# One transfer of 2 MB for each expert weight matrix, in place of two of 1 MB

## What is computed

```
def expert_block(args):
    xb, e = args
    return (jax.nn.silu(xb @ w_gate[e]) * (xb @ w_up[e])) @ w_down[e]
# w_gate, w_up: (32, 1024, 512); w_down: (32, 512, 1024), float32: 2 MB each matrix, 6 MB an expert
```

## Time and profile before

| | |
|---|---|
| median of 3 runs | 1305.73 us (1301.58 to 1308.01) |
| the profiled execution | 1303.58 us, of which the span from first to last instruction is 1301.7 us |
| PE busy | 1159.6 us (89%) |
| DVE busy | 888.3 us (68%) |
| ACT busy | 738.4 us (57%) |
| DMA queue of SP (q1) | 241.83 MB, 49.1% of the 16 engines' time |
| DMA queue of ACT (q10) | 25.17 MB, 5.8% |
| weights of experts | 192 transfers of 1024 KB; median from issue to landing 8.2 us (down) to 9.6 us (gate) |

### The profile page before, as it was taken

How to read it: one execution, slowest core, us unless ns; L and a number is a source line. 1 busy time by engine, 2 the same in 40 slices (tenths; PEclk the granted TensorE clock), 3 DMA queues, 4 the chain that set the end, 5 groups by cost and what they waited for, 6 DMA issues and landing times. The chain is left out here.

```text
span 1301.7 us, 17793 instructions
## 1 busy us (share of the span) xinstructions
PE 1159.6 (89%) x6109; PEld 907.0 (70%) x6109; DVE 888.3 (68%) x1117; ACT 738.4 (57%) x882; POOL 80.0 (6%) x135
## 2 busy tenths in 40 slices
PE   5999999999999997799849999999999999999930
PEld 3888788779878885588736666766666766667620
DVE  7345635543563454666668889888898888988828
ACT  7344444453444434523247777777777777777714
POOL 0011011011010000011200000000000000000013
PEclk9999999999999998899969999999999999999975
DMA  6145353355341000584359999999999999999838
GB/s 181 50 114 123 81 129 81 89 122 120 89 98 40 17 18 1 200 322 159 150 202 377 383 393 392 404 395 388 390 395 398 400 390 392 390 397 400 316 97 333
DMA packets 86215, 306.31 MB, mean 235 GB/s; under 512 B 14664, under 2 KB 39240, under 8 KB 61600
## 3 DMA queue, kind: packets, MB, share of 16 engines
q1 hardware_dynamic: 67680, 241.83, 49.1%
q0 software_dynamic: 11328, 38.80, 10.8%
q10 hardware_dynamic: 7168, 25.17, 5.8%
HBM read 254.36 MB, written 51.41 MB: 235 GB/s over the span
## 5 line engine op out<-in xcount | busy, mean ns | idle before, releaser
L1476 DVE TENSOR_TENSOR m_wl<-raw,m_wh 128x2048 fp32r<-128x2048 f32 x192 | 437.2, 2289 | 74.8 <-ACT m_wh L1350 72.3
L1350 ACT ACTIVATE m_wh<-raw 128x2048 fp32r<-128x2048 f32 x192 | 367.9, 1918 | 130.1 <-PE m_py L131 50.6
L129 PE MATMUL m_pg<-m_wh,m_xh 128*96 128x512 f32 x256 | 104.2, 407 | 6.6 <-DVE m_xl L1480 5.3
L143 PE MATMUL a_pj<-zh,a_wh 128*128 128x348 f32 (+1 forms) x416 | 107.5, 355 | 0.5 <-DVE a_wl L495 0.5
L143 PE MATMUL a_pj<-zl,a_wh 128*128 128x348 f32 (+1 forms) x416 | 107.6, 355 | 0.0
L143 PE MATMUL a_pj<-zh,a_wl 128*128 128x348 f32 (+1 forms) x416 | 106.4, 352 | 0.0
L129 PE MATMUL m_py<-m_wh,m_hh 128*96 128x512 f32 x256 | 102.5, 401 | 2.3 <-DVE m_hl L1505 2.3
L129 PE MATMUL m_pu<-m_wh,m_xh 128*96 128x512 f32 x256 | 102.7, 401 | 0.0
L131 PE MATMUL m_pg<-m_wh,m_xl 128*96 128x512 f32 x256 | 101.7, 397 | 0.0
L130 PE MATMUL m_pg<-m_wl,m_xh 128*96 128x512 f32 x256 | 101.3, 396 | 0.0
L131 PE MATMUL m_pu<-m_wh,m_xl 128*96 128x512 f32 x256 | 101.2, 395 | 0.0
(11 more groups left out here) (241 smaller groups left out, 2107.1 us busy)
## 6 DMA issues: line engine op xcount, KB each, us to landing
raw<-in_w_gate_dram SPq DMA_DIRECT2D x64, 1024.0 KB, 9.6
raw<-in_w_up_dram SPq DMA_DIRECT2D x64, 1024.0 KB, 8.9
raw<-in_w_down_dram SPq DMA_DIRECT2D x64, 1024.0 KB, 8.2
xrows<-a_kl POOLq DMA_DIRECT2D x51, 256.0 KB, 4.9
a_raw<-in_w_in_dram SPq DMA_DIRECT2D x24, 512.0 KB, 4.0
m_xg<-xrows ACTq DMA_DIRECT2D x32, 384.0 KB, 8.1
yrows<-m_ys ACTq DMA_DIRECT2D x32, 384.0 KB, 6.9
yrows<-a_kl POOLq DMA_DIRECT2D x33, 256.0 KB, 4.9
```

What stands on the lines that cost most here:

```text
L129: nc.tensor.matmul(out, xh, wh, start=first, stop=False)
L143: mm = nc.tensor.matmul(out, w[:, k, 0:m], z[:, k, at:at + n], start=n_pass == 0, stop=n_pass == PASSES - 1)
L1350: nc.scalar.activation(wh[s][:], raw[j][:], ACT.Copy).then_inc(S["w_hi"], 1)
L1476: nc.vector.tensor_tensor(wl[s][:], raw[j][:], wh[s][:].bitcast(F32), ALU.subtract).then_inc(S["w_lo"], 1)
```

## The change

Each matrix becomes one transfer of 2 MB, 16 KB in each partition, into one of three staging buffers `big[0]` to `big[2]`. The units stay as they were for ACT, DVE and PE: `raw[j]` is now the first or second half of `big[j // 2]`. Both halves' `high` wait for the landing of the whole matrix, and SP waits for the `low` of the second half before it issues the next transfer into the buffer. The transfers ahead in the router stage are three instead of six, with the same bytes in the same order.

```diff
-                        for e, kind, j in [(0, 0, 2), (0, 1, 3), (0, 2, 4), (0, 3, 5), (1, 0, 0), (1, 1, 1)]:
-                            to, src = unit(c.raw[j], kind, e, w_gate, w_up, w_down)
+                        for e, m, j in [(0, 0, 1), (0, 1, 2), (1, 0, 0)]:
+                            to, src = matrix(c.big[j], m, e, w_gate, w_up, w_down)
                             sp.dma_start(to, src).then_inc(c.raw_in[j], 16)
...
-def unit(raw, j, e, w_gate, w_up, w_down):
-
-    n, w = (DE, (w_gate, w_up)[j // 2]) if j < 4 else (D, w_down)
-    half = UNIT // n
-    rows = w[0, bass.ds(e, 1), :, :].rearrange("o (p k) n -> p (o k) n", p=P)
-    return raw[:].rearrange("p (k n) -> p k n", n=n), rows[:, (j % 2) * half:(j % 2 + 1) * half, :]
+def matrix(raw, m, e, w_gate, w_up, w_down):
+
+    n, w = (D, w_down) if m == 2 else (DE, (w_gate, w_up)[m])
+    return raw[:].rearrange("p (k n) -> p k n", n=n), w[0, bass.ds(e, 1), :, :].rearrange("o (p k) n -> p (o k) n", p=P)
...
-                    for kind in kinds(shift):
+
+                    for kind in kinds(shift)[::2]:
...
-                            sp.wait_ge(S["w_lo"], split(N, j - UNITS))
-                        to, src = unit(raw[j], kind, behind if kind in DOWN else e, w_gate, w_up, w_down)
-                        sp.dma_start(to, src).then_inc(raw_in[j], 16)
+                            sp.wait_ge(S["w_lo"], split(N, j + 1 - UNITS))
+                        to, src = matrix(c.big[j // 2], kind // 2, behind if kind in DOWN else e, w_gate, w_up, w_down)
+                        sp.dma_start(to, src).then_inc(raw_in[j // 2], 16)
...
-                    act.wait_ge(raw_in[j], N * 16 + (16 if j >= 2 else 0))
+                    act.wait_ge(raw_in[j // 2], N * 16 + (16 if j >= 2 else 0))
...
-            c.raw = [c.sb(ctx, f"raw{j}", [P, UNIT], F32) for j in range(UNITS)]
-            c.raw_in = [c.sem(f"first_raw_in{j}") for j in range(UNITS)]
+            c.big = [c.sb(ctx, f"raw{j}", [P, 2 * UNIT], F32) for j in range(UNITS // 2)]
+            c.raw = [c.big[j // 2][:, j % 2 * UNIT:(j % 2 + 1) * UNIT] for j in range(UNITS)]
+            c.raw_in = [c.sem(f"first_raw_in{j}") for j in range(UNITS // 2)]
```

More of the change, by code:

```diff
@@ L1217, in experts @@
                                               "y_copied", "ids_ready", "counted", "made", "placed", "collected", "listed", "own", "passed")}
-        raw_in = [c.sem(f"{tag}_raw_in{j}") for j in range(UNITS)] if dynamic else c.raw_in
+        raw_in = [c.sem(f"{tag}_raw_in{j}") for j in range(UNITS // 2)] if dynamic else c.raw_in
         gathered = [c.sem(f"{tag}_gathered{s}") for s in range(2)]
@@ L1346, in high @@
                     s = (UNITS * u + j) % RING
-                    act.wait_ge(raw_in[j], N * 16 + (16 if j >= 2 else 0))
+                    act.wait_ge(raw_in[j // 2], N * 16 + (16 if j >= 2 else 0))
                     act.wait_ge(S["unit_used"], N * UNITS + (j + 1))
-                    nc.scalar.activation(wh[s][:], raw[j][:], ACT.Copy).then_inc(S["w_hi"], 1)
+                    nc.scalar.activation(wh[s][:], raw[j], ACT.Copy).then_inc(S["w_hi"], 1)
                 def x_high(N, u):
@@ L1475, in low @@
                     dve.wait_ge(S["w_hi"], N * UNITS + (j + 1))
-                    nc.vector.tensor_tensor(wl[s][:], raw[j][:], wh[s][:].bitcast(F32), ALU.subtract).then_inc(S["w_lo"], 1)
+                    nc.vector.tensor_tensor(wl[s][:], raw[j], wh[s][:].bitcast(F32), ALU.subtract).then_inc(S["w_lo"], 1)
                 def x_low(N, u):
```

## The result

| | before | changed |
|---|---|---|
| median (22 runs each) | 1304.39 us | 1308.02 us |
| range | 1301.18 to 1309.34 | 1302.78 to 1312.27 |
| profiled execution, span | 1301.7 us | 1306.2 us |
| last matmul of the experts | 1250.4 us | 1254.6 us |

The ratio is 1.0029 with a 95% interval of 1.0018 to 1.0039: the changed kernel is slower by 3.8 us (3.6 by the medians), less than half a per cent, but clear of the noise. Measured again beside other kernels it was 1.0028 (1.0016 to 1.0040) and 1.0034 (1.0020 to 1.0049). The time lies in the range that was predicted; the forecast of no change at all, though, was wrong, and a sum of 0 us has to be explained against 4.

What follows compares the result with a forecast made beforehand. The prediction took PE to bound the experts' stage, with transfers just keeping up. Its terms summed to 0 us, giving 1305.7 us, the median of the three runs, with a range of 1299 to 1314 us.

Steps and rivals of the forecast that it cites:

- PE bounds the stage; the transfers just keep up.: Experts' stage: PE busy 99.7 of 100 us sets the pace, not the DMA share of 1.02.
- The landing: Weight transfers: the matrix's last byte arrives when now, leaving 1.8, 0.9 and 1.2 us before the first highs; cost 0.
- Runs of 16 KB: Weight transfers: longer runs were taken to move at the 8 KB rate, 426 GB/s with full queue.
- If the margin is gone: From ACT's highs to PE: a single landing may be 5.3 us late before PE stops.
- The dry bound: Weight transfers, each meeting an empty queue: landing 11.1 us, over the 17.96 us step only for UP, costing 0 to 5 us.
- The point of decision: Landing time beyond which a lost head start would cost: 11.3 us for DOWN, 10.9 us for UP and GATE.
- rival 1: Weight transfers: first half's head start lost in full, +1.4 us an expert, 43 us, 1348 us; chance 8 in 100.
- Rival 2: DMA beside ACT's row stores: mixing costs 0.95 us more an expert, 28 us, 1334 us; chance 6 in 100.
- Rival 3: Experts' stage bound by DMA: steady 426 GB/s shortens it by 39 us, 1266 us; chance 6 in 100.
- What the profile would show: Experts' stage if right: step 17.96 us, waits on PE as now, landings 9 to 11.3 us, highs 0 to 2 us later.
- Both signs of being wrong: Experts' stage: landings over 11.3 us in the steady state, or the DMA share falling while the step grows.
- The resolution: Whole-kernel timing: a measurement was said to tell about 0.5%, 6.5 us, from no change.

Runs made afterwards that it cites:

- e7: Kernel before, with ACT splitting rows between GATE's halves and DVE doing `m_xl` between GATE's two lows; ratio 0.9941, median 1295.8 us.
- e15: Kernel before with late issue of both halves and ACT waiting for both landings, still two transfers of 1 MB (a repeat); ratio 0.9998.
- e14: Changed kernel with 64 bytes between a staging buffer's halves, so one 2 MB transfer in runs of 8 KB (a repeat); ratio 1.0010.
- e13: The changed kernel again, unedited, measured on one chip beside two variants; ratio 1.0034 against the kernel before.
- e6: Changed kernel, with ACT splitting rows between GATE's halves and DVE doing `m_xl` between GATE's two lows; ratio 1.0013, step 18.01 us.
- e11: Kernel before with rows split between GATE's halves, late issue and whole landing together, two transfers of 1 MB; ratio 0.9985, step 17.85 us.
- e2: Kernel before, with only ACT's high of a first half waiting for the landing of both halves; ratio 0.9994.
- e3: Kernel before with late issue of both halves and ACT waiting for both landings, still two transfers of 1 MB; ratio 0.9987.
- e4: Changed kernel with 64 bytes between a staging buffer's halves, so one 2 MB transfer in runs of 8 KB; ratio 1.0006.
- e5: The changed kernel again, unedited, measured beside other kernels; ratio 1.0028 against the kernel before.

## Why the prediction was wrong

- *"PE bounds the stage; the transfers just keep up."* Right for PE's waits. But the way by which PE is bound was read from matmul rhythm and from the weights' slots alone. PE also waits 0.2 us at each start of GATE for `m_xl`, and no view that I used names this: the wait is shorter than what the waits' list shows for PE and stands there only as "PEld m_pg <- issue". Of the 7.7 us that e7 gains (0.59%), 6.2 lie at the 30 turns to GATE and were there to be seen, and 1.5 at the first two experts.
- *The landing: "the last byte of the matrix arrives when the second half's does now, because the bytes ahead of it are the same".* This step failed. The term was 9.0, 10.3 and 9.6 us for UP, DOWN and GATE; measured 10.4, 11.3 and 11.3. Against what was left, 1.8, 0.9 and 1.2 us, that is 1.4, 1.0 and 1.7 us more: UP keeps a margin (0.5 us in the trace), DOWN and GATE have none. With two transfers of 1 MB the step does hold: from the end of the second `low`, DOWN takes 10.6 us in e15 and 10.5 before. One transfer of 2 MB takes 11.1 us in runs of 8 KB (e14) and 11.6 in runs of 16 KB (e13).
- *"Runs of 16 KB ... I take the 8 KB rate."* Failed too, though not by the rate of the weights themselves: the row transfers on ACT's queue become late, 10.0 instead of 8.3 us, and around each row load 0.13 to 0.17 MB less is moved. The two bounds looked at the rate of the weights alone and left the other queue out. "If the hardware cuts the 16 KB up again" did not happen, as the packets show.
- *"If the margin is gone ... late by 5.3 us before PE stops."* This step failed as well and is what turned late landings into lost time. It followed the late high only to the matmuls that use those weights, and there it may well be right: the first low of GATE ends 4 us before its first matmul even in the changed kernel. On ACT the row split `m_xh` stands behind the highs of GATE, on DVE `m_xl` stands behind their lows and `m_hid`, and there the margin was 0 us, as the chain shown above tells. e6 and e7 show this way, by removing it.
- *The dry bound: 11.1 us landing at most, "0 to 5 us".* The bound was passed (11.3 to 11.5 us). The cost of 3.8 us lies within what it allowed, but by luck: the 5 us were worked out for UP, which waits for nothing. Hold and landing were the right pair to add up, for DOWN: its hold shrinks to 6.44 us when both halves are split back to back, and with 0.18 us to the issue, 11.34 to the landing and 0.10 to the high (medians of the changed kernel) the cycle has 18.06 us, the step. That says that no slack is left in it; it doesn't explain the landing.
- *The point of decision in rival 1, "a landing takes more than 11.3 us (DOWN)".* This was the right kind of number, and the changed kernel sits on it (11.3 us; with the shorter hold of 6.44 us, and 0.3 us for issue and start, the point is 11.2). The mechanism of rival 1, a lost head start, is real only together with the whole landing and only at a faster pace (e11). The price of 43 us was far too high: it took the whole delay as lost, while in e15 none of it was.
- *Rival 2, mixing with the row transfers.* Nearest to what happened, with the load instead of the store: the slow time around the load is 6 us, where it is 5 before and 4 in e14 with runs of 8 KB. The rate beside the store stays at 421 to 430 GB/s. Its price of 28 us took a loss of 0.95 us of DMA time a step; measured are 0.3 to 0.4 us (against e14), and the step grew by 0.1.
- *Rival 3* (a stage bound by DMA gains from larger transfers) did not occur: nothing became faster, and the rate of 391 GB/s, from 394, is that of the same bytes in a longer step. So the sentence of the Trainium skill (DMA: Bandwidth & Descriptors, section Bandwidth) on larger batches, set beside it then, found no support in this case.
- *What the profile would show* had "landings 9 to 11.3 us" and "each first high 0 to 2 us after its landing". DOWN and GATE have 0.1 us, which is what a wait looks like. Both signs of being wrong came true: DOWN lands after 11.3 to 11.5 us, and the DMA share fell (1.01 to 1.02 before, 1.00 to 1.01 changed) while the step grew.
- *The resolution, "about 0.5%, 6.5 us".* It was set too coarse. With 22 runs each the interval is 0.2% wide, and a loss of 0.3% is seen.

What stays open: why one transfer of 2 MB lands later than two of 1 MB issued together (11.1 against 10.6 us from the same event, the same bytes in runs of 8 KB; up to 0.2 us of it may be the longer issue, and the bytes are asked for in another order, both runs of a partition together). Open too is why the weights move slower beside a row load, and why for longer when they come in long runs; no experiment changed the row load alone without changing its bytes. Landing times also depend on more than the edits: in e2, whose issues are those of the kernel before, DOWN's second halves land after 8.9 us instead of 10.4, and no run says why. Repeated kernels do agree (e3 and e15, e4 and e14, the three of the changed kernel, within 0.12 us for DOWN). Also, in which steps PE loses its time changes from one execution to the next: mostly before 900 us in the first trace of the changed kernel, mostly after it in e5 (98.27 of 100 us at 900 to 1000).

## What to carry to other kernels

Follow a wait through every instruction behind it on its engine, and from there through the other engines' queues, not only to the work that uses the awaited data: here the token rows stood behind the second half of the weights, which was needed 2.8 us later than they were, and putting them first was worth 0.6%. A staging buffer that is filled and freed as a whole has a cycle of landing plus hold; look at it when both of its overlaps, early issue of a part and early use of a part, are to be given up together (here 0.4%, and only at a step of 17.7 us; at 17.95 us nothing). And when runs are made longer on one DMA queue, look at the landings of the other queues: here, with DMA full, 384 KB landed 1.7 to 1.9 us later, at the same bytes.

## What was not expected of the hardware

A transfer's run length shows in another queue's landing times: with weights in runs of 16 KB instead of 8 KB, loads of 384 KB on ACT's queue land after 10.0 instead of 8.3 us and stores after 8.5 instead of 6.6 (e13 against e14), and around each row load the core moves 0.13 to 0.17 MB less. The packets of weights themselves take the same time for a byte. And the same 2 MB issued as one transfer land 0.5 us later than as two that are issued half a us apart, counted from the same event (e14 against e15, DOWN).
